# Selected-keys attention by groups of three heads, with fp32r logits and one wide values product

## The chip, the cores and the metric

The kernel runs on one core of a Trainium2 chip. The metric is the device time of one execution in microseconds (us). TensorE (PE) multiplies and transposes into PSUM, its weight loads are shown as PEld, VectorE is DVE, ScalarE is ACT, GpSimd is POOL, and SyncE (SP) issues the weight stream. TensorE's clock has two levels, 1.2 and 2.4 GHz; the profile gives it as a granted share, 0.50 or 1.00. fp32r is a float32 with fewer mantissa bits, which TensorE takes in one pass; a plain fp32 product takes four.

## What is computed

The reference is two transformer blocks over 1024 tokens of width 1024. The change touches one part of the first block, the selected-keys attention (six heads of 64 in two key groups, 128 queries at a time, 256 selected keys per query):

```
# one block of 128 queries
score = einsum('bqh,bqhs->bqs', wi_b, relu(einsum('bqhd,bsd->bqhs', qi_b, ki))) * idx_scale
score = where(causal, score, -inf)
_, sel = top_k(score, topk)                      # topk = 256
logits = einsum('bqgrd,bqkgd->bqgrk', qg, k_sel) * HEAD_DIM ** -0.5   # g: 2 groups, r: 3 heads
logits = where(valid, logits, -inf)
p = softmax(logits, axis=-1)
o = einsum('bqgrk,bqkgd->bqgrd', p, v_sel)
```

Everything else (projections, convolutions, memory attention, feed-forward, the second block) is computed by both kernels in the same way.

## The kernel before

All projections are weight-streaming products: SyncE loads a tile of weights, GpSimd splits it into two fp32r parts (`w_hi`, `w_lo`, lines 425 and 427), and TensorE multiplies them by the two parts of the activations (lines 516 to 520). Each engine has its own program, written out in order; they meet at semaphores, and in `meet` (line 383) all three wait for each other.

The attention is done densely. The scores of the index heads are reduced to a mask by 32 rounds of eight maxima (`topk_round`, line 1618), which VectorE runs beside the convolution tiles and the gate tiles. Then `L1694` turns the taken scores to 0 and the others to -1e30, the engines meet, and the stage that I call DSA begins: 48 steps, one for each block `i` of 128 queries and each head (`DSA_PLAN`), from 128 keys for block 0 to 1024 for block 7. A step n runs through the engines so:

- PE (lines 801 to 821): the logits of step n (`L809`, plain fp32, 64 rows, one or two banks of `side`), the transposes of the probabilities of step n-1 (`L736`, in `probs_turn`), the values product of step n-2 (`L819`, plain fp32, 128 columns for each key block).
- DVE (1697 to 1713): adds the mask and takes the row maximum into a strip `T` (`L1704`), negates it (`L1708`), waits for the exponential, inverts the sum (`L1710`), scales the strip (`L1712`).
- ACT (1192 to 1209): the exponential with its row sum (`L1196`), the copy of the transposed strips (`L1134`, in `copy_turned`), the head's output (`L1204`), and after six heads the rounding of the block (`L1208`); POOL takes the low part (`L486`).

Ahead of the stage ACT fetches the spilled gates (`fetch`) and the second memory input (`m_in`); behind it come the tiles of the attention's output projection. The convolution (`L1653` to `L1672` on DVE) and the gates (`gate_blocks`) stand before it.

## Time and profile before

| | us |
|---|---|
| median of 3 runs | 3167.75 (3165.0 to 3170.51) |
| the profiled execution | 3164.58 |
| its span | 3162.5 |
| PE busy | 2957.7 (94%) |
| DVE busy | 1713.8 (54%) |
| ACT busy | 768.3 (24%) |
| POOL busy | 1158.9 (37%) |
| mean granted clock of TensorE | 0.959 |

The views used further on are these. The page's chain follows the work that ended last back to the start. The stretches give the busy time of each engine between two times, with the granted clock. The timeline gives single instructions in order of time; "idle before" in brackets is how long the engine stood and who ended it. The groups by line give the mean duration of one instruction. A TensorE duration in a timeline contains the pipeline's tail, so what one matmul costs in a stream is the distance from start to start, or its share in the chain.

### The profile page before, as it was taken

The page shows a single profiled execution, that of the slowest core. Times are in us where ns is not written, and L with a number is a line of the kernel's source. Part 1 is how long each engine was busy: PE and PEld are TensorE (multiplying, and loading weights), DVE is VectorE, ACT ScalarE, POOL GpSimd, SP SyncE. Part 2 cuts the span into 40 slices and gives each one's busy share as a digit, 9 for nine tenths or more (in the row PEclk, how much of TensorE's full clock was granted, in tenths as well). Part 3 has the DMA queues.
Part 4 walks back from the last instruction along what each step waited for, and adds up shares of the span by engine and source line. Part 5 has one row for each costly group of instructions (what it writes and reads, how often), then busy time and mean ns, then how long its engine had stood idle before and what let it go on. Part 6 is the DMA issues. An engine that isn't in the chain of part 4 may idle for free.

```text
span 3162.5 us, 35461 instructions
## 1 busy us (share of the span) xinstructions
PE 2957.7 (94%) x13362; PEld 2385.8 (75%) x13362; DVE 1713.8 (54%) x2369; ACT 768.3 (24%) x1389; POOL 1158.9 (37%) x649
## 2 busy tenths in 40 slices
PE   7987999998989899999999879999888999999997
PEld 4675878885767688888888667887666888888885
DVE  4475899985552633242332647888948333333327
ACT  3054011113531311020110255666613000000002
POOL 2330434441023333344334415555532443334331
PEclk9978999996999999999999989999999999999998
DMA  3110112221031111111111210000020111111111
GB/s 144 41 34 7 47 67 80 80 80 67 1 133 67 34 47 54 47 46 46 53 46 47 67 74 27 21 27 27 21 80 27 54 47 47 52 46 46 47 53 60
DMA packets 45053, 165.40 MB, mean 52 GB/s; under 512 B 4880, under 2 KB 6160, under 8 KB 43920
## 3 DMA queue, kind: packets, MB, share of 16 engines
q1 hardware_dynamic: 37168, 129.31, 12.3%
q10 hardware_dynamic: 7776, 34.61, 2.8%
q8 instruction: 72, 1.18, 0.1%
q14 instruction: 37, 0.30, 0.0%
HBM read 147.12 MB, written 16.78 MB: 52 GB/s over the span
## 4 chain that ended last, share of the span: by engine, by line
PE 82%; DVE 11%; issue 3%; ACT 2%; DVEq 1%; POOL 0%; ACTq 0%; DMA 0%; SPq 0%; POOLq 0%
PE dense L516 21%; PE dense L520 20%; PE dense L517 20%; DVE stay L1914 2%; PE dense L904 2%; PE side L809 2%; PE dense L905 2%; PE dense L906 2%; PE dense L819 1%; DVE a_lo L1521 1%; PE dense L736 1%; PE dense L553 1%; PE side L942 1%; PE dense L554 1%; PE dense L555 1%
## 5 line engine op out<-in xcount | busy, mean ns | idle before, releaser
L425 POOL TENSOR_TENSOR w_hi<-raw,zero 128x1024 fp32r<-128x1024 f32 x210 | 401.1, 1910 | 1584.3 <-PE dense L520 1327.0
L516 PE MATMUL dense<-a_hi,w_hi 128*128 128x512 f32 x2000 | 786.0, 393 | 32.6 <-DVE T L1820 8.2
L517 PE MATMUL dense<-a_lo,w_hi 128*128 128x512 f32 x2000 | 781.9, 391 | 0.0
L520 PE MATMUL dense<-a_hi,w_lo 128*128 128x512 f32 x2000 | 618.9, 391 | 0.0
L427 POOL TENSOR_TENSOR w_lo<-raw,w_hi 128x1024 fp32r<-128x1024 f32 x210 | 524.9, 2499 | 16.5
L516 PEld LDWEIGHTS dense<-a_hi,w_hi 128*128 128x128 f32 x2000 | 378.2, 189 | 115.1 <-issue 14.9
L517 PEld LDWEIGHTS dense<-a_lo,w_hi 128*128 128x128 f32 x2000 | 378.1, 189 | 79.5 <-issue 1.2
L520 PEld LDWEIGHTS dense<-a_hi,w_lo 128*128 128x128 f32 x2000 | 377.5, 189 | 79.0
L516 PE MATMUL dense<-b_hi,w_hi 128*128 128x512 f32 x832 | 326.8, 393 | 4.0 <-DVE T L1820 2.5
L517 PE MATMUL dense<-b_lo,w_hi 128*128 128x512 f32 x832 | 324.4, 390 | 0.0
L1800 DVE TENSOR_TENSOR x_res<-x_res,dense 128x1024 f32<-128x1024 f32 x100 | 122.0, 1220 | 328.4 <-PE dense L520 327.0
L1820 DVE SCALAR_TENSOR_TENSOR T<-dense,tiny,T 128x1023 f32<-128x1023 f32 x88 | 112.8, 1282 | 295.1 <-ACT T L1259 291.6
L520 PE MATMUL dense<-b_hi,w_lo 128*128 128x512 f32 x832 | 256.7, 390 | 0.0
L475 POOL TENSOR_TENSOR stick_weights<-stick_weights,stay 128x511 f32<-128x511 f32 (+2 forms) x144 | 132.0, 917 | 174.8 <-DVE stay L1914 174.8
L516 PEld LDWEIGHTS dense<-b_hi,w_hi 128*128 128x128 f32 x832 | 156.4, 188 | 44.9 <-issue 4.8
L1411 ACT ACTIVATE b_hi<-T 128x1024 fp32r<-128x1024 f32 x32 | 34.0, 1062 | 610.1 <-DVE T L1995 610.1
L520 PEld LDWEIGHTS dense<-b_hi,w_lo 128*128 128x128 f32 x832 | 156.5, 188 | 32.8
L517 PEld LDWEIGHTS dense<-b_lo,w_hi 128*128 128x128 f32 x832 | 156.5, 188 | 31.7
L1259 ACT ACTIVATE T<-dense,tiny 128x1024 f32<-128x1024 f32 x44 | 49.2, 1117 | 518.5 <-PE dense L520 514.5
L1624 DVE MATCH_REPLACE8 score<-tiny,score 128x384 f32<-128x384 f32 (+2 forms) x192 | 165.7, 876 | 0.0
L1620 DVE MAX8 tiny<-score 128x8 f32<-128x384 f32 (+2 forms) x192 | 155.4, 877 | 3.1 <-issue 1.9
L1993 DVE TENSOR_SCALAR T<-dense 128x1024 f32<-128x1024 f32 x32 | 39.2, 1224 | 191.6 <-PE dense L520 190.6
(263 smaller groups left out, 4406.8 us busy)
## 6 DMA issues: line engine op xcount, KB each, us to landing
raw<-in_w_stream SPq DMA_DIRECT2D x231, 512.0 KB, 3.4
x_in<-in_x_t SPq DMA_DIRECT2D x8, 512.0 KB, 7.2
spill_gate<-T ACTq DMA_DIRECT2D x8, 512.0 KB, 2.6
spill_part<-gates ACTq DMA_DIRECT2D x8, 512.0 KB, 2.7
back<-spill_gate ACTq DMA_DIRECT2D x8, 512.0 KB, 3.8
back<-spill_part ACTq DMA_DIRECT2D x8, 512.0 KB, 4.8
x_res<-in_x_t ACTq DMA_DIRECT2D x2, 2048.0 KB, 9.5
spill_x<-x_res ACTq DMA_DIRECT2D x1, 4096.0 KB, 13.6
```

What stands on the lines that cost most here:

```text
L425: pool.tensor_tensor(w_hi[:, r % 2, :], raw[:, r, :], zero[:, 0:1].broadcast_to([P, D]), ALU.add).then_inc(weights_rounded, 1)
L427: pool.tensor_tensor(w_lo[:, r % 2, :], raw[:, r, :], w_hi[:, r % 2, :].bitcast(F32), ALU.subtract).then_inc(weights_split, 1)
L475: pool.tensor_tensor(w[:, 0:width - 1], w[:, 0:width - 1], stay[n % STRIPS][:, 1:width], ALU.mult).then_inc(w_ready, 1)
L516: pe.matmul(o, w_hi[:, slot, w], hi[:, k, x], start=b == 0, stop=False)
L517: pe.matmul(o, w_hi[:, slot, w], lo[:, k, x], start=False, stop=False)
L520: last = pe.matmul(o, w_lo[:, slot, w], hi[:, k, x], start=False, stop=stop)
L809: last = pe.matmul(side[:, n % 2, c:e], q_f[r, h % 3, i * P:i * P + P], k_f[r, c:e], start=True, stop=True)
L904: pe.matmul(o, w_hi[:, t % 2, w], a_hi[:, b, x], start=b == 0, stop=False)
L1620: dve.max(best[:, i - TOPK // P, :], score[:, score_at(i):score_at(i + 1)])
L1624: dve.match_replace(sc, best[:, i - TOPK // P, :], sc, TAKEN)
L1800: dve.tensor_tensor(x_res[:, n, :], x_res[:, n, :], dense[:, u % 2, :], ALU.add).then_inc(sums_free[u % 2], 1)
L1820: last = dve.scalar_tensor_tensor(T[:, slot, d:S], dense[:, u % 2, 0:S - d], tap, T[:, slot, d:S], ALU.mult, ALU.add)
```

## The change

DSA now goes by groups of three heads that share keys and values (16 groups: block `i`, key group `g`), and in a second kind of step, the turn: one key block of one group, 72 in all.

- Logits: the keys of a group are rounded to fp32r and stored above their own remainder (`k_stack`, 128 rows). The queries are rounded (`round_queries`, ACT) and their remainder is taken (`split_queries`, DVE), each written twice, for both halves of the rows. A head's logits are then two fp32r products over 128 rows instead of one fp32 product over 64 (`att_logits`).
- Turns: `att_turn` transposes one key block of three heads into one bank, one copy of 384 columns takes it to `pt` (every third on DVE, the others on ACT), and `att_values` multiplies it, plain fp32, with 384 columns, two turns later.
- Strips: nine of them, so maxima and exponentials run ahead of the turns. The first three groups are masked before the first turn; group s has its logits spread over the turns of group s-2 (`LOGITS_AT`), and its queries are rounded and split one turn before its first logits (`DUP_AT`).
- The mask (before: one instruction ahead of the barrier) is made in the stage, block by block. `m_in` is loaded after the stage. The keys and the first two groups of queries are split before the convolution and before the gates.

The diff, without tile allocations, semaphore names and two changed arguments:

```diff
@@ -92,8 +92,33 @@
 IDX_STEPS = (TB - TOPK // P) * IDX_H
-DSA_PLAN = [(i, h) for i in range(TB) for h in range(ATT_H)]
+DSA_PLAN = [(i, g) for i in range(TB) for g in range(GROUPS)]
 DSA_STEPS = len(DSA_PLAN)
+REP = ATT_H // GROUPS
+DSA_TURNS = [(s, kb) for s, (i, g) in enumerate(DSA_PLAN) for kb in range(i + 1)]
+DSA_X0 = [DSA_TURNS.index((s, 0)) for s in range(DSA_STEPS)] + [len(DSA_TURNS)]
+DSA_LEAD, DSA_LAG, DSA_STRIPS = 3, 2, 9
+def logits_at(s, j):
+    first, last = DSA_X0[s - 2] - 1, DSA_X0[s - 1] - 2
+    return first + (last - first) * j // (REP - 1)
+LOGITS_AT = {}
+for _n in range(REP * DSA_LEAD, REP * DSA_STEPS):
+    LOGITS_AT.setdefault(logits_at(_n // REP, _n % REP), []).append(_n)
+DUP_AT = {logits_at(s, 0) - 1: s for s in range(DSA_LEAD + 2, DSA_STEPS)}
+def on_dve(x):
+    return x % 3 == 2
+def copies_before(x):
+    return (x // 3, x - x // 3)[0 if on_dve(x) else 1]
 IDX_S = S - TOPK
...
@@ -798,27 +847,51 @@
-            for n in range(DSA_STEPS + 2):
-                if n < DSA_STEPS:
-                    i, h = DSA_PLAN[n]
-                    r = slice(HD * (h // 3), HD * (h // 3) + HD)
-                    if n >= 2:
-                        pe.wait_ge(lg_max, TB + n - 1)
-                    for c in range(0, P * (i + 1), 512):
-                        e = min(P * (i + 1), c + 512)
-                        last = pe.matmul(side[:, n % 2, c:e], q_f[r, h % 3, i * P:i * P + P], k_f[r, c:e], start=True,
-                                         stop=True)
-                    last.then_inc(lg_ready, 1)
-                if 1 <= n <= DSA_STEPS:
-                    probs_turn(n - 1, TB, DSA_PLAN[n - 1][0] + 1)
+            pe.wait_ge(k_low, GROUPS)
+            def att_logits(n):
+                s, j = n // REP, n % REP
+                i, g = DSA_PLAN[s]
+                pe.wait_ge(dup_split, s + 1)
                 if n >= 2:
-                    b = n - 2
-                    i = DSA_PLAN[b][0]
-                    pe.wait_ge(lg_tc, TB + b + 1)
-                    for kb in range(i + 1):
-                        last = pe.matmul(dense[:, b % 2, 0:P], v_f[:, kb, :], T[:, 2 + b % 2, kb * P:kb * P + P],
-                                         start=kb == 0, stop=kb == i)
-                    last.then_inc(lg_o, 1)
+                    pe.wait_ge(d_max, n - 1)
+                for c in range(0, P * (i + 1), 512):
+                    e = min(P * (i + 1), c + 512)
+                    pe.matmul(side[:, n % 2, c:e], qd_hi[:, s % 2, j, :], k_stack[:, g, c:e], start=True, stop=False)
+                    last = pe.matmul(side[:, n % 2, c:e], qd_lo[:, s % 2, j, :], k_stack[:, g, c:e], start=False, stop=True)
+                last.then_inc(d_ready, 1)
+            def att_turn(x):
+                s, kb = DSA_TURNS[x]
+                if kb == 0:
+                    pe.wait_ge(d_probs, REP * (s + 1))
+                if x >= 2:
+                    probs_copied(pe, x - 2)
+                for j in range(REP):
+                    last = pe.transpose(att_turn_bank(x)[:, j * P:j * P + P],
+                                        strips[(REP * s + j) % DSA_STRIPS][:, kb * P:kb * P + P], ident[:, :])
+                last.then_inc(d_turned, 1)
+            def att_values(x):
+                s, kb = DSA_TURNS[x]
+                if kb == 0 and s >= 2:
+                    pe.wait_ge(d_taken, s - 1)
+                probs_copied(pe, x)
+                pe.matmul(att_out_bank(s), v_f[:, kb, :], pt[:, x % 4, :], start=kb == 0, stop=kb == DSA_PLAN[s][0]
+                          ).then_inc(d_out, 1)
+            for n in range(REP * DSA_LEAD):
+                att_logits(n)
+            for x in range(len(DSA_TURNS) + DSA_LAG):
+                if x < len(DSA_TURNS):
+                    att_turn(x)
+                for n in LOGITS_AT.get(x, ()):
+                    att_logits(n)
+                if x >= DSA_LAG:
+                    att_values(x - DSA_LAG)
             meet(pe, "pe", met_n)
...
@@ -1140,6 +1213,17 @@
+            def round_queries(s):
+                i, g = DSA_PLAN[s]
+                if s >= 2:
+                    act.wait_ge(d_ready, REP * (s - 1))
+                for half in (g, 1 - g):
+                    last = act.activation(qd_hi[group_rows(half), s % 2, :, :], q_f[group_rows(g), :, i * P:i * P + P], ACT.Copy)
+                last.then_inc(dup_round, 1)
+            for g in range(GROUPS):
+                act.activation(k_stack[group_rows(g), g, :], k_f[group_rows(g), :], ACT.Copy).then_inc(k_round, 1)
             for j in range(3):
...
@@ -1148,6 +1232,9 @@
                 act.activation(yc_hi[:, j, :], T[:, 2, :], ACT.Copy).then_inc(parts["yc"][0], 1)
+            act.wait_ge(parts["yc"][1], 3)
+            for s in range(2):
+                round_queries(s)
...
@@ -1188,27 +1275,44 @@
             fetch(1)
-            act.dma_start(m_in[:, :, :], io["mem2_t"]).then_inc(mem2_loaded, 16)
-            for n in range(DSA_STEPS + 2):
-                if n < DSA_STEPS:
-                    w, e = P * (DSA_PLAN[n][0] + 1), n % 8
-                    act.wait_ge(lg_max, TB + n + 1)
-                    act.activation(T[:, n % 2, 0:w], T[:, n % 2, 0:w], ACT.Exp, bias=neg_max[:, e:e + 1], scale=SCALE,
-                                   accum_out=row_sum[:, e:e + 1]).then_inc(lg_exp, 1)
-                if 1 <= n <= DSA_STEPS:
-                    copy_turned(n - 1, TB, P * (DSA_PLAN[n - 1][0] + 1))
-                if n >= 2:
-                    i, h = DSA_PLAN[n - 2]
-                    r = slice(HD * (h // 3), HD * (h // 3) + HD)
-                    act.wait_ge(lg_o, TB + n - 1)
-                    act.activation(ya_f[r, h % 3, i * P:i * P + P], dense[r, n % 2, 0:P], ACT.Copy).then_inc(lg_oc, 1)
-                    if h == ATT_H - 1:
-                        act.wait_ge(lg_oc, TB + n - 1)
+            def exponentials(n):
+                w, e = P * (DSA_PLAN[n // REP][0] + 1), n % 8
+                act.wait_ge(d_max, n + 1)
+                act.activation(strips[n % DSA_STRIPS][:, 0:w], strips[n % DSA_STRIPS][:, 0:w], ACT.Exp, bias=neg_max[:, e:e + 1],
+                               scale=SCALE, accum_out=row_sum[:, e:e + 1]).then_inc(d_exp, 1)
+            for s in range(DSA_LEAD):
+                for j in range(REP):
+                    exponentials(REP * s + j)
+                    if j == 0:
+                        round_queries(s + 2)
+            for x in range(len(DSA_TURNS) + DSA_LAG + 1):
+                if x < len(DSA_TURNS) and not on_dve(x):
+                    act.wait_ge(d_turned, x + 1)
+                    if x >= 4:
+                        act.wait_ge(d_out, x - 3)
+                    act.activation(pt[:, x % 4, :], att_turn_bank(x), ACT.Copy).then_inc(d_copied_act, 1)
+                for n in LOGITS_AT.get(x, ()):
+                    exponentials(n)
+                if x in DUP_AT:
+                    round_queries(DUP_AT[x])
+                e = x - DSA_LAG - 1
+                if e >= 0 and e + 1 in DSA_X0:
+                    s = DSA_X0.index(e + 1) - 1
+                    i, g = DSA_PLAN[s]
+                    act.wait_ge(d_out, e + 1)
+                    act.activation(ya_f[group_rows(g), :, i * P:i * P + P],
+                                   att_out_bank(s)[group_rows(g), :].rearrange("p (j q) -> p j q", j=REP), ACT.Copy
+                                   ).then_inc(d_taken, 1)
+                    if g == GROUPS - 1:
+                        act.wait_ge(d_taken, s + 1)
                         act.activation(ya_hi[:, :, i * P:i * P + P], ya_f[:, :, i * P:i * P + P], ACT.Copy
+            act.dma_start(m_in[:, :, :], io["mem2_t"]).then_inc(mem2_loaded, 16)
...
@@ -1650,6 +1754,19 @@
+            def split_queries(s):
+                i, g = DSA_PLAN[s]
+                dve.wait_ge(dup_round, s + 1)
+                for half in (g, 1 - g):
+                    last = dve.tensor_tensor(qd_lo[group_rows(half), s % 2, :, :], q_f[group_rows(g), :, i * P:i * P + P],
+                                             qd_hi[group_rows(g), s % 2, :, :].bitcast(F32), ALU.subtract)
+                last.then_inc(dup_split, 1)
+            for g in range(GROUPS):
+                dve.wait_ge(k_round, g + 1)
+                dve.tensor_tensor(k_stack[group_rows(1 - g), g, :], k_f[group_rows(g), :],
+                                  k_stack[group_rows(g), g, :].bitcast(F32), ALU.subtract).then_inc(k_low, 1)
             for j in range(3):
...
@@ -1670,6 +1787,8 @@
                 low((yc_hi[:, j, :], yc_lo[:, j, :]), j, T[:, 2, :], "yc", j + 1)
+            for s in range(2):
+                split_queries(s)
...
@@ -1690,27 +1809,53 @@
-            sc = score[:, score_at(2):score_at(TB)]
-            dve.tensor_scalar(sc, sc, TAKEN / 2, NEG, ALU.is_gt, ALU.mult)
             meet(dve, "dve", met_n)
-            for n in range(DSA_STEPS):
-                i, e = DSA_PLAN[n][0], n % 8
+            def mask(n):
+                s, e = n // REP, n % 8
+                i = DSA_PLAN[s][0]
                 w = P * (i + 1)
-                dve.wait_ge(lg_ready, TB + n + 1)
-                if n >= 2:
-                    dve.wait_ge(lg_t, TB + n - 1)
-                dve.tensor_tensor_reduce(out=T[:, n % 2, 0:w], in0=side[:, n % 2, 0:w],
-                                         in1=score[:, score_at(i):score_at(i) + w], scale=1.0, scalar=TAKEN, op0=ALU.add,
-                                         op1=ALU.max, accum_out=row_max[:, e:e + 1])
+                sc = score[:, score_at(i):score_at(i) + w]
+                if i >= TOPK // P and n % (REP * GROUPS) == 0:
+                    dve.tensor_scalar(sc, sc, TAKEN / 2, NEG, ALU.is_gt, ALU.mult)
+                    dve.drain()
+                dve.wait_ge(d_ready, n + 1)
+                if s >= 3:
+                    dve.wait_ge(d_turned, DSA_X0[s - 2])
+                dve.tensor_tensor_reduce(out=strips[n % DSA_STRIPS][:, 0:w], in0=side[:, n % 2, 0:w], in1=sc, scale=1.0,
+                                         scalar=TAKEN, op0=ALU.add, op1=ALU.max, accum_out=row_max[:, e:e + 1])
                 dve.drain()
-                dve.tensor_scalar(neg_max[:, e:e + 1], row_max[:, e:e + 1], -SCALE, None, ALU.mult).then_inc(lg_max, 1)
-                dve.wait_ge(lg_exp, TB + n + 1)
+                dve.tensor_scalar(neg_max[:, e:e + 1], row_max[:, e:e + 1], -SCALE, None, ALU.mult).then_inc(d_max, 1)
+            def normalise(n):
+                w, e = P * (DSA_PLAN[n // REP][0] + 1), n % 8
+                dve.wait_ge(d_exp, n + 1)
                 dve.reciprocal(inv_sum[:, e:e + 1], row_sum[:, e:e + 1])
                 dve.drain()
-                dve.tensor_scalar(T[:, n % 2, 0:w], T[:, n % 2, 0:w], inv_sum[:, e:e + 1], None, ALU.mult
-                                  ).then_inc(lg_p, 1)
+                dve.tensor_scalar(strips[n % DSA_STRIPS][:, 0:w], strips[n % DSA_STRIPS][:, 0:w], inv_sum[:, e:e + 1], None,
+                                  ALU.mult).then_inc(d_probs, 1)
+            for n in range(REP * DSA_LEAD + 2):
+                if n < REP * DSA_LEAD:
+                    mask(n)
+                    if n % REP == 0:
+                        split_queries(n // REP + 2)
+                if n >= 2:
+                    normalise(n - 2)
+            for x in range(len(DSA_TURNS)):
+                if on_dve(x):
+                    dve.wait_ge(d_turned, x + 1)
+                    if x >= 4:
+                        dve.wait_ge(d_out, x - 3)
+                    dve.tensor_copy(pt[:, x % 4, :], att_turn_bank(x)).then_inc(d_copied_dve, 1)
+                for n in LOGITS_AT.get(x, ()):
+                    mask(n)
+                for n in LOGITS_AT.get(x - 1, ()):
+                    normalise(n)
+                if x in DUP_AT:
+                    split_queries(DUP_AT[x])
             meet(dve, "dve", met_n)
```

The order of TensorE before, in block 7: logits of a head, transposes of the one before, values of the one before that. `side` holds logits, `T` probabilities, `v_f` values.

```order
L809 MATMUL side<-k_f,q_f 128x512 [waits row_max_ready]
L809 MATMUL side<-k_f,q_f 128x512
L736 MATMUL dense<-ident,T 128x128 [waits heads_copied,probs_ready]
L736 MATMUL dense<-ident,T 128x128 x7
L819 MATMUL dense<-T,v_f 128x128 [waits probs_copied]
L819 MATMUL dense<-T,v_f 128x128 x6
```

The order of TensorE now, from the last head of the fourteenth group (896 keys) to the first of the fifteenth (1024 keys): `strip` holds probabilities, `att_probs_t` the copied turns, `qd_hi` and `qd_lo` the queries.

```order
L861 MATMUL side<-k_stack,qd_hi 128x512 [waits att_row_max_ready,queries_split]
L862 MATMUL side<-k_stack,qd_lo 128x512
L861 MATMUL side<-k_stack,qd_hi 128x384
L862 MATMUL side<-k_stack,qd_lo 128x384
L883 MATMUL dense<-att_probs_t,v_f 128x384 [waits att_probs_copied_dve]
L873 MATMUL dense<-ident,strip_108 128x128 [waits att_probs_copied_act]
L873 MATMUL dense<-ident,strip_109 128x128
L873 MATMUL dense<-ident,strip_110 128x128
L861 MATMUL side<-k_stack,qd_hi 128x512 [waits att_row_max_ready,queries_split]
L862 MATMUL side<-k_stack,qd_lo 128x512
```

One turn of values and transposes stands between the last logits of a group and the next group's, which wait for `queries_split`.

The order of VectorE before, one head of 896 keys and the start of the next (`ISA` is the masking with its maximum):

```order
L1704 ISA T,tiny<-side,score 128x896 [waits probs_turned,logits_ready]
L1704 ISA tiny 128x1
L1708 TENSOR_SCALAR tiny<-tiny 128x1
L1710 RECIPROCAL tiny<-tiny 128x1 [waits exp_ready]
L1712 TENSOR_SCALAR T<-T,tiny 128x896
L1704 ISA T,tiny<-side,score 128x896 [waits probs_turned,logits_ready]
```

The order of VectorE now, at the same two heads as TensorE's rows, from the last head of 896 keys to the first of 1024:

```order
L1826 ISA strip_107,tiny<-side,score 128x896 [waits att_probs_turned,att_logits_ready]
L1826 ISA tiny 128x1
L1829 TENSOR_SCALAR tiny<-tiny 128x1
L1762 TENSOR_TENSOR qd_lo<-q_f,qd_hi 64x384 [waits queries_rounded]
L1762 TENSOR_TENSOR qd_lo<-q_f,qd_hi 64x384
L1852 COPY att_probs_t<-dense 128x384 [waits att_values_done,att_probs_turned]
L1821 TENSOR_SCALAR score<-score 128x1024
L1826 ISA strip_108,tiny<-side,score 128x1024 [waits att_probs_turned,att_logits_ready]
L1826 ISA tiny 128x1
L1829 TENSOR_SCALAR tiny<-tiny 128x1
L1835 RECIPROCAL tiny<-tiny 128x1 [waits att_exp_ready]
L1837 TENSOR_SCALAR strip_107<-strip_107,tiny 128x896
```

The split of the next group's queries stands between the maximum of the last head and its normalisation, and waits for `queries_rounded`; on ScalarE the rounding stands behind that head's exponential.

## Rows read from the trace of the kernel before

**Rows 1.** The page, part 4: shares of the chain that ended last, by engine.

```profile
PE 82%; DVE 11%; issue 3%; ACT 2%; DVEq 1%; POOL 0%; ACTq 0%; DMA 0%; SPq 0%; POOLq 0%
```

**Rows 2.** Stretches: us, busy us and instructions by engine, PE clock, DMA.

```profile
735.10:796.80 61.70, 57.15 (x167) 36.45 (x168) 24.12 (x105) 27.33 (x85) 2.98 (x3) 0.50 0.15 55
796.80:904.80 108.00, 103.92 (x626) 75.69 (x626) 52.49 (x135) 58.81 (x117) 4.99 (x5) 1.00 0.00 1
```

**Rows 3.** Chain, at the lower and full clock: start us, us, what.

```profile
767.82 0.85 PE dense L819 x4
...
858.06 0.92 PE dense L736 x7
858.97 1.56 PE dense L819 x14
860.54 1.70 PE side L809 x4
```

**Rows 4.** Timeline of a head: start us, us, engine, line, what, idle.

```profile
849.96 1.09 DVE L1704 CUSTOM_DVE_ANT_0 T<-side,score 128x896 f32<-128x896 f32 x1 [0.38 <-PE side L809]
851.32 1.04 ACT L1196 ACTIVATE T<-T,tiny 128x896 f32<-128x896 f32 x1 [1.57 <-DVE tiny L1708]
852.48 0.16 DVE L1710 RECIPROCAL tiny<-tiny 128x1 f32<-128x1 f32 x1 [1.20 <-ACT T L1196]
852.73 0.69 DVE L1712 TENSOR_SCALAR T<-T,tiny 128x896 f32<-128x896 f32 x1
```

**Rows 5.** By line, 600 to 1200 us: busy us, mean ns, idle.

```profile
L1704 DVE CUSTOM_DVE_ANT_0 T<-side,score 128x1024 f32<-128x1024 f32 x6 | 7.3, 1224 | 5.2 <-PE side L809 5.2
L1704 DVE CUSTOM_DVE_ANT_0 T<-side,score 128x128 f32<-128x128 f32 x6 | 1.7, 288 | 1.5 <-PE side L809 1.5
L1196 ACT ACTIVATE T<-T,tiny 128x1024 f32<-128x1024 f32 x6 | 6.9, 1149 | 12.7 <-DVE tiny L1708 12.7
L1196 ACT ACTIVATE T<-T,tiny 128x128 f32<-128x128 f32 x6 | 2.4, 401 | 4.6 <-DVE tiny L1708 4.6
L1712 DVE TENSOR_SCALAR T<-T,tiny 128x1024 f32<-128x1024 f32 x6 | 4.5, 753 | 0.8 <-issue 0.4
L1712 DVE TENSOR_SCALAR T<-T,tiny 128x128 f32<-128x128 f32 x6 | 1.7, 287 | 0.5
L1208 ACT ACTIVATE ya_hi<-ya_f 128x384 fp32r<-128x384 f32 x8 | 4.2, 524 | 0.2
L1830 DVE TENSOR_TENSOR b_lo<-T,b_hi 128x1024 fp32r<-128x1024 f32 x4 | 4.9, 1225 | 4.5 <-ACT b_hi L1264 4.5
```

**Rows 6.** A stretch of the gates, PE in fp32r only.

```profile
480.00:560.00 80.00, 80.00 (x355) 66.26 (x354) 78.50 (x131) 7.94 (x12) 34.43 (x16) 1.00 0.24 83
```

**Rows 7.** Timeline where the stage begins.

```profile
730.54 4.49 DVE L1694 TENSOR_SCALAR score<-score 128x4224 f32<-128x4224 f32 x1
730.65 0.34 ACTq L1175 DMA_DIRECT2D spill_part<-gates  x1
737.85 1.28 ACT L1196 ACT_TABLE_LOAD   x1 [15.93 <-issue]
```

**Rows 8.** Stretches in and behind two gaps of PE.

```profile
403.70:407.80 4.10, 0.00 (x0) 0.00 (x0) 4.06 (x9) 0.00 (x0) 3.85 (x2) 0.98 0.00 0
409.30:414.70 5.40, 5.36 (x13) 4.24 (x14) 4.54 (x4) 0.43 (x1) 0.00 (x0) 0.52 0.27 97
902.70:904.80 2.10, 0.02 (x1) 0.00 (x0) 0.00 (x0) 0.79 (x2) 0.99 (x1) 1.00 0.00 0
906.00:909.20 3.20, 3.20 (x10) 2.44 (x9) 0.00 (x0) 0.00 (x0) 0.00 (x0) 0.50 0.00 0
```

**Rows 9.** The page, part 6: issues, KB each, us to landing.

```profile
spill_part<-gates ACTq DMA_DIRECT2D x8, 512.0 KB, 2.7
```

**Rows 10.** VectorE's waits in the two stages ahead.

```profile
327.65 1.22 DVE L1659 TENSOR_TENSOR T<-dense,T 128x1024 f32<-128x1024 f32 x1 [3.92 <-PE dense L520]
...
448.90 1.22 DVE L1685 TENSOR_TENSOR gates<-dense,gates 128x1024 f32<-128x1024 f32 x1 [1.67 <-PE dense L520]
```

25 lines of the change are left out of this document (22 added, 3 removed).

## The prediction, made before the result was known

> **What bounds the kernel now.** I read first the page's chain: TensorE (PE) carries 82% of what ended last [rows 1]. A change elsewhere counts only where PE waits for it. Then the stretches [rows 2]: the stage of the change (DSA, the selected-keys attention) runs from 735.1 to 904.8 us, 169.7 us, with VectorE busy 76.6 us and ScalarE 86.1 us. Up to 796.8 PE's granted clock is 0.50 (1.2 GHz), after it 1.00 (2.4 GHz). In the chain of that stage [rows 3] a head of 896 keys is 0.92 us of transposes, 1.56 of values, 1.70 of logits, end to end: 4.18 us, all PE. At the low level two blocks of values take 0.85, twice as long each. So PE bounds each head here: the four-pass fp32 products do, not the waits. Last the timeline of one head [rows 4]: row maximum at 849.96, exponential from 851.32, reciprocal at 852.48, probabilities ready at 853.42. VectorE sits 1.20 us behind the exponential in each head. Before the change that is hidden, since PE has the last head's values and the next head's logits to do.
>
> **What each piece costs.** Linear in width between the rows for 128 and 1024 keys [rows 5]:
> - M, logits ready to maximum ready: 0.29 to 1.22 for the reduction, 0.23 for accumulator and negation (849.96 to 851.32, less 1.09 and a hop of 0.04 [rows 4]): 0.52 to 1.46.
> - E, maximum ready to VectorE's reciprocal: the exponential plus 0.16 (851.32 to 852.48 for one of 1.04, and the hop): 0.56 to 1.31.
> - N, the normalisation: 0.25 to its start [rows 4] and 0.29 to 0.75: 0.54 to 1.00.
> - R, round_queries: two ScalarE copies of 64x384. The nearest row, 128x384, has 0.52: 1.0. Bounds: 0.8 (two at the 0.40 of a 128-wide exponential) to 1.2.
> - S, split_queries: two VectorE subtractions of 64x384. 1024 columns take 1.23; less 640 at the reduction's 1.04 ns each leaves 0.56: 1.12. Bounds: 0.6 (the 128-wide reduction's 0.29 a piece) to 2.5 (1.23 a piece).
> - A copy of turned strips, 128x384 out of PSUM: 0.5 on ScalarE, by the same row of 0.52; on VectorE 0.55, where the reduction, also a read of PSUM, has 384 columns.
> - L, logits of one head in fp32r: PE does 355 matmuls of 512 in 80 us at the full clock [rows 6], 0.225 each, so four are 0.90 for 1024 keys, where fp32 took 1.70 for 896. About 0.2 for 128 keys.
> - A turn (one key block, three heads): transposes 3 x 0.13 = 0.39, values 3 x 0.22 less the saved loads = 0.65: 1.04. The bounds of the 384-column product are 0.34 (two records at an fp32r matmul's 0.44 ns a column) and 0.67; I take 0.65, because the fp32 block of 128 is the same arithmetic.
>
> Sums: PE has 72 turns x 1.04 = 75 and 27648 columns of logits in two passes, 25: 100 us at the full clock. VectorE has 48 heads at (M + N + 0.05), 83; 24 copies, 13; 14 splits, 16; the score mask, 5: 117. ScalarE is near 98. By totals alone the stage would be 120 to 140 us. That is not what the order of the instructions gives.
>
> **The new wait.** The queries of a group are rounded and split right behind the last head of the group before, and the logits of the new group wait for that (queries_split). The rows of the order show it. The chain for each group from the sixth to the last, eleven times, is: L, then 0.2 until VectorE starts, M, E, R, S, 0.1 for two hops, and only then the next logits. For 1024 keys: 0.9 + 0.2 + 1.46 + 1.31 + 1.0 + 1.12 + 0.1 = 6.1 us; for 512: 4.7. Behind its last logits PE has one values product and one turn's transposes (1.04 us), and then its next matmul is the waiting one: it idles 6.1 - 0.9 - 1.04 = 4.1 us at 1024, about 3.2 at 512. Queued behind it are all turns, values and copies of the stage. The rounding is queued behind the exponential, the split behind the rounding, so nothing overlaps. In the chain of before no piece passes another: transposes, values and logits of three different heads follow in the order written [rows 3].
> The Trainium skill ("TensorE: Matmul & The Clock Gate", Part 2, step 1) says that only weight loads are pulled ahead while matmuls stay in program order. By that rule the turns behind the wait can't fill the gap and the sum stands; if PE could pass it, 11 gaps of some 3.7 us, 40 us, would go. The trace agrees with the rule.
>
> A second, smaller coupling: ScalarE's copy of turn x+1 stands behind the exponential of turn x, and the transposes of turn x+3 need it. From the logits of one head to those of the next, three turns later, at 1024: 0.9 + 0.2 + 1.46 + 1.31 + 0.5 (copy) + 0.4 (transposes) = 4.8 us, where PE alone has 0.9 + 3 x 1.04 = 4.0.
>
> **The sum, at the full clock.** Time from a group's first logits to the next group's:
> - 384 keys: two M of 0.79, one N of 0.67, a copy's share (2.6) and the chain of 4.4: 7.0
> - 512: two (M + N) of 0.92 + 0.74, 3.4 with hops, the chain 4.7, copy and mask 0.6: 8.7
> - 640: two M and three N, 4.7, the chain 5.2, copy and mask 0.8: 10.7
> - 768: two heads that VectorE walks through one by one (M + E + N = 3.2 each), 6.4 + 5.5 + 0.4 = 12.3
> - 896: to the third head's logits 1.0, then one M + E + N of 3.5 and one wait for ScalarE's copy of 3.5, 8.1; the chain 5.8: 13.9
> - 1024: two of the 4.8 above and the chain of 6.1: 15.7
>
> Before, three heads took 3 x 4.18 = 12.5 us at 896. The groups of 384 keys once, 512 to 896 twice each and 1024 once make 7.0 + 2 x (8.7 + 10.7 + 12.3 + 13.9) + 15.7 = 114. Ahead stands the lead-in, VectorE's: 15 maxima (six of 128, six of 256, three of 384 keys, 10.5 with the hops), 14 normalisations (8), four splits (4.5), one copy and twice a wait for logits (2), and its waits for ScalarE: 3.2 at the first split, because the DMA issues and the table load of 1.28 [rows 7] stand before the first exponential, and 5 for later roundings: 33 us. At the end the last group's heads (9.6), then its last logits, 17 turns, one wait for a copy and the last two values (0.9 + 17.7 + 1 + 1.3 = 21), and the same 2.1 us from PE's end to the next stage as before [rows 8]. Total 33 + 114 + 9.6 + 21 + 2.1 = 180 us, 10 more than before, though PE's own work is down to 100 us.
>
> **The clock.** The rows [rows 8] show what such gaps do: idle 403.7 to 409.3, then 0.50 until about 414.7; idle 902.7 to 904.8, then 0.50 from 906.0 to 909.2. So after a gap of 3 to 4 us I expect some 4.4 us at 1.2 GHz (the rows have 3.2 and 5.4), in which PE does half: 2.2 lost, a little of it covered by ScalarE's copies, 1.9 net. Nine groups: 17. The two smallest groups fit into the slow stretch whole, 3 more. Total 20, so the stage is 200 us.
>
> **The edits around it.** The score mask, 4.49 us of VectorE alone before the barrier [rows 7], moves into the stage. Instead the barrier waits for the spill issued at 730.65, 2.7 us to landing [rows 9]: it opens near 733.4, not 735.1, a gain of 1.7. Splitting the keys (two 64x1024, 2.5 us and the wait for ScalarE) ends before VectorE's wait of 3.92 us for PE; the first two query splits (3.3) fall on its wait of 1.67 before the first gate product and on the one behind it [rows 10]. PE waits for neither: zero, at most 2. Loading mem2 after the stage costs ScalarE an issue while it waits: zero; at most 1 if it delays the fetches.
>
> Profiled execution before: 3164.58. Stage +30.3, barrier -1.7: 3193.2. The median shown is 3.2 above that execution: **3196**.
>
> A second rule: "VectorE: DVE Perf Modes", section "Why PSUM operands drop a tier", in the Trainium skill, gives a copy out of PSUM the single rate, where one inside SBUF may go double. My row agrees: the normalisation in SBUF grows by 0.52 ns a column, the reduction from PSUM by 1.04. At the SBUF rate the 24 copies would be 3 us less, which moves no case.
>
> **Rivals.**
> 1. The clock holds at 2.4 GHz through the gaps. For: from 796.8 to 904.8 it held, with PE busy 103.9 of 108 us, so short waits leave it alone [rows 2]. Against: gaps of 2 and 4 us did not [rows 8]. Stage 180, 3176.
> 2. The clock stays at 1.2 GHz throughout, as from 735 to 797, where PE was busy 57 of 61.7 us and it did not rise [rows 2]. Periods are then PE's doubled work plus the gap: 8.1, 11.0, 14.3, 17.0, 20.0, 23.1; with tail: 247. 3243.
> 3. Faster: the split chain doesn't bind, because rounding and splitting cost near their lower bounds and exponentials hide behind turns; then the engines' totals bind (VectorE 117 plus the end on PE, 140). 3136. It decides if the chain takes under about 2 us more than the turns it stands beside. For: the totals. Against: every link is a measured duration in a fixed order.
> 4. The change does nothing that counts: chain and saved logits cancel, within 6 us of before. It needs the chain 1 us shorter in each group and no clock loss.
>
> **Chances.** Mine 0.46 (alone 3180 to 3215), rival 1 0.18, rival 2 0.11, rival 3 0.19, rival 4 0.06. Faster or slower means by over 0.2%, 6 us, about what a measurement tells: faster 0.19, same 0.06, slower 0.75. The range must hold rival 1, most of 2 and the bounds of R and S (11 x 1 us down, 11 x 1.6 up): 3150 to 3242.
>
> **What would show it.** Right: in the stage's waits PE idles behind the query split (about eleven times, 3 to 4 us, at its logits), VectorE behind ScalarE's rounding; the stage lasts near 200 us with PE under 75% busy, its clock switching in each group; logits of 512 at 0.23 us apart. Wrong: a stage under 165 us, VectorE over 80% busy in it, or no PE wait over 2 us.

## The result, and the profile after

The changed kernel takes 3191.62 us (median of 4 runs, 3189.02 to 3193.12), the kernel before 3168.66 (4 runs): ratio 1.0070, 95% interval 1.0058 to 1.0083, 18 to 26 us slower. The predicted time was 3196, and slower had 0.75. The profiled execution took 3191.37 us, span 3189.5.

The page's chain [rows 1] reads, after the change:

```profile
PE 81%; DVE 11%; issue 3%; ACT 3%; DVEq 1%; POOL 0%; DMA 0%; ACTq 0%; SPq 0%; POOLq 0%
```

All shares are within a point of those before, so that line hides what happened. The stretches of the stage [rows 2] show it (us, busy us and instructions of PE, PEld, DVE, ACT, POOL, granted clock, DMA share, GB/s):

```profile
735.00:758.00 23.00, 9.77 (x32) 7.65 (x33) 12.75 (x61) 10.91 (x31) 0.00 (x0) 0.50 0.32 114
758.00:798.00 40.00, 27.04 (x102) 19.19 (x102) 28.24 (x91) 21.90 (x54) 2.01 (x2) 0.80 0.00 1
798.00:890.00 92.00, 62.81 (x250) 43.26 (x249) 52.52 (x126) 42.52 (x86) 4.00 (x4) 0.85 0.00 1
890.00:920.10 30.10, 26.15 (x127) 16.77 (x125) 10.54 (x23) 13.53 (x27) 1.99 (x2) 1.00 0.02 3
735.00:920.10 185.10, 125.76 (x505) 86.87 (x505) 104.05 (x298) 88.86 (x197) 8.01 (x8) 0.82 0.04 15
```

The stage takes 185.1 us instead of 169.7, although PE is busy 35 us less than before (125.8 against 161.1). PE's waits in it (engine, tile, line, released by: us in total, times, longest):

```profile
PE side L861 <- DVE qd_lo L1762: 40.3, 11, 4.5
PE side L861 <- DVE tiny L1829: 13.1, 8, 4.4
PE side L861 <- ACTq L435: 5.9, 1, 5.9
PE dense L873 <- ACT att_probs_t L1296: 3.4, 3, 1.8
```

The first row is the new wait of the prediction, eleven times. One of its chains from the trace, for 896 keys, to be read beside the head of before [rows 4] (start us, us, engine, line, what, idle before and its releaser):

```profile
862.98 0.48 PE L861 MATMUL side<-k_stack,qd_hi 128*128 128x512 f32 x1
...
864.09 1.09 DVE L1826 CUSTOM_DVE_ANT_0 strip<-side,score 128x896 f32<-128x896 f32 x1 [0.28 <-PE side L862]
...
864.53 0.49 PE L873 MATMUL dense<-ident,strip 128*128 128x128 f32 x3
...
865.45 1.04 ACT L1283 ACTIVATE strip<-strip,tiny 128x896 f32<-128x896 f32 x1 [1.49 <-DVE tiny L1829]
...
866.49 1.04 ACT L1222 ACTIVATE qd_hi<-q_f 64x384 fp32r<-64x384 f32 x2
867.57 1.12 DVE L1762 TENSOR_TENSOR qd_lo<-q_f,qd_hi 64x384 fp32r<-64x384 f32 x2 [2.15 <-ACT qd_hi L1222]
...
868.74 0.50 PE L861 MATMUL side<-k_stack,qd_hi 128*128 128x512 f32 x1 [3.72 <-DVE qd_lo L1762]
```

Logits, maximum, exponential, rounding, split, logits: 5.76 us from 862.98 to 868.74, where the prediction's pieces give 5.8. PE's last work in it is three transposes at 864.53, then nothing for 3.72 us. For 1024 keys the chain is 6.25 (880.18 to 886.43, predicted 6.1) and the idle time 4.10 (predicted 4.1).

The stage explains 15.4 us, not all 27.0 that lie between the two spans. Ahead of it nothing is left over: 735.2 and 735.0. Behind it the kernel before and the changed one read:

```profile
904.86:3162.50 2257.64, 2134.77 (x9684) 1743.41 (x9684) 1084.88 (x1286) 526.68 (x915) 896.66 (x522) 0.97 0.15 51
```
```profile
920.10:3189.50 2269.40, 2143.99 (x9684) 1748.42 (x9684) 1086.42 (x1286) 527.65 (x915) 896.97 (x522) 0.97 0.15 51
```

The counts are the same on every engine, the code is the same, and it takes 11.8 us longer. PE is busy 9.2 us longer with the same 9684 matmuls, so most of it is slower matmuls; the other 2.6 us are waits, in small pieces. The same gap of PE in both, in the feed-forward, and what follows it (stretch, its length, PE busy and matmuls, granted clock, DMA share, GB/s), before and after:

```profile
1072.10:1080.30 8.20, 0.00 (x1) 0.78 0.39 128
1080.30:1082.80 2.50, 2.46 (x6) 0.50 0.00 0
1082.80:1085.30 2.50, 2.50 (x11) 0.86 0.00 0
```
```profile
1091.55:1099.75 8.20, 0.00 (x1) 0.69 0.41 130
1099.75:1102.25 2.50, 2.46 (x6) 0.50 0.00 0
1102.25:1104.75 2.50, 2.50 (x8) 0.50 0.00 0
```

The gap is 8.2 us in both. Behind it the clock comes back after some 3 us in the one and not within 5 us in the other: 17 matmuls in 5 us against 14. Reading the granted clock in slices of 2.5 us over the whole part, it was at 0.50 for 113 us in all before and for 135.5 us after. PE works at half its speed in that time, so half of the difference, 11.3 us, is about the time that is missing. The prediction had no such term.

### The profile page after: what moved, and what is told of

The parts are those of the page before. It is cut to its first block, busy times and chain, and to the rows that moved or that the text cites. A ratio compares the mean times of both kernels' runs of the same rounds, so it can differ in the third digit from the quotient of the medians.

```text
span 3189.5 us, 35000 instructions
## 1 busy us (share of the span) xinstructions
PE 2932.1 (92%) x13074; PEld 2366.9 (74%) x13074; DVE 1740.1 (55%) x2432; ACT 776.6 (24%) x1391; POOL 1158.4 (36%) x649
## 3 DMA queue, kind: packets, MB, share of 16 engines
q1 hardware_dynamic: 37168, 129.31, 12.1%
q8 instruction: 70, 1.15, 0.1%
## 4 chain that ended last, share of the span: by engine, by line
PE 81%; DVE 11%; issue 3%; ACT 3%; DVEq 1%; POOL 0%; DMA 0%; ACTq 0%; SPq 0%; POOLq 0%
PE dense L565 21%; PE dense L566 20%; PE dense L569 20%; DVE stay L2059 2%; PE dense L977 2%; PE dense L978 2%; PE dense L979 2%; PE dense L602 1%; DVE a_lo L1625 1%; PE dense L603 1%; PE dense L604 1%; PE side L1015 1%; PE dense L883 1%; ACT T L1187 1%; PE side L635 1%
```

## The experiments

Numbers of the stage run from PE's first logits to the first product of the output projection, as above. "Low" is the time that the granted clock was at 0.50, from slices of 2.5 us.

**Is the chain the cause? The duplication one group earlier** (with this, PE's program is unchanged; ScalarE and VectorE round and split behind the first head of the group before).

```
-DUP_AT = {logits_at(s, 0) - 1: s for s in range(DSA_LEAD + 2, DSA_STEPS)}
+DUP_AT = {logits_at(s - 1, 0): s for s in range(DSA_LEAD + 2, DSA_STEPS)}
```

> The rounding and the split of a group's queries are issued behind the first head of the group before, not behind its last one; nothing else is moved. Theory 1 (the serial chain from a group's last logits to the next group's first is what PE waits for, 11 times, 40 us in the trace of the changed kernel): the waits of PE behind qd_lo (L1762) nearly go, below 5 us in sum. What comes next is VectorE, which now stands behind the exponential and the rounding inside the group before (2.3 us a time, of which about half is in PE's shadow), so some 25 of the 40 us come back: stage 160 us, kernel near 3166. Rival (the wait only shows where VectorE, ScalarE and PE together would be late anyway): the idle time moves to the transposes and the logits behind row maxima, and the stage stays within 5 us of 185: 3187 or more.

Measured: 3164.25 us, ratio to before 0.9982 (0.9973 to 0.9992), stage 162.5, low 32 us of it (66 in the changed kernel). PE's waits in the stage:

```profile
PE dense L873 <- ACT att_probs_t L1296: 20.1, 19, 2.7
PE side L861 <- DVE tiny L1829: 15.5, 11, 4.3
PE dense L873 <- DVE att_probs_t L1852: 6.7, 5, 2.0
...
PE side L861 <- DVE qd_lo L1762: 1.6, 1, 1.6
```

One line of the plan takes 22.6 us out of the stage and turns a loss of 0.7% into a gain of 0.2%. The wait for the split falls from 40.3 to 1.6 us; the rival is out. What came next is not VectorE, as I expected, but the prediction's second coupling: transposes that wait for a copy which ScalarE issues behind an exponential.

**Ahead of the exponential and the maximum too.**

```
                 for n in LOGITS_AT.get(x, ()):
-                    exponentials(n)
-                if x in DUP_AT:
-                    round_queries(DUP_AT[x])
+                if x in DUP_AT:  round_queries(DUP_AT[x])      # and on VectorE split_queries before mask
+                for n in ...:    exponentials(n)
```

> As the run with the early rounding and split, but within their step they also stand ahead of the exponential and of the row maximum, so that they wait for no new logits. Theory 1: VectorE waits for the rounding only (1.0 us), in a stretch in which PE has turns to do: stage 150 us, kernel near 3156. Rival (the engines' coupling sets the pace, whatever the place of the split): within 5 us of the changed kernel, 3187.

Measured: 3174.80 us, ratio 1.0008 (0.9998 to 1.0018), stage 171.5, low 60. I expected a stage of 150: a miss. PE's largest waits:

```profile
PE dense L873 <- ACT att_probs_t L1296: 23.2, 12, 4.3
PE side L861 <- DVE tiny L1829: 19.9, 12, 4.5
```

VectorE's waits for the rounding are still 18.9 us in all (from 760 us on), and they now stand ahead of the maxima. The move only changed what waits: rounding and split (1.04 + 1.12) now stand between the logits and their maximum, the exponential comes that much later, and the copy behind it too. Waits of up to 4.3 us at the transposes let the clock fall, as the chain's had.

**One half alone: grouped turns, plain fp32 logits.**

```
-pe.matmul(side[:, n % 2, c:e], qd_hi[:, s % 2, j, :], k_stack[:, g, c:e], start=True, stop=False)
-last = pe.matmul(side[:, n % 2, c:e], qd_lo[:, s % 2, j, :], k_stack[:, g, c:e], start=False, stop=True)
+last = pe.matmul(side[:, n % 2, c:e], q_f[group_rows(g), j, i * P:i * P + P], k_f[group_rows(g), c:e],
+                 start=True, stop=True)      # and no rounding, no split, no wait for them
```

> One half of the change alone: groups of three heads, 384-column values product and copies by two engines, but the logits stay a plain fp32 product of the 64-row queries and keys; keys and queries are neither rounded nor split. Theory 1: no chain, PE has 75 us of turns and 27648 columns at 1.9 ns, 52 us, 127 at the full clock; with a lead-in of some 25 us that runs partly beside it and at the low level the stage takes 150 to 155 us, kernel near 3158, below the kernel before (3168). Rival: the grouped turns themselves cost (copies of 384 columns on a path that is blocked by exponentials), then the stage stays at 175 or more, 3180.

Measured: 3179.41 us, ratio 1.0024 (1.0014 to 1.0035), stage 175.7. The theory (150 to 155) missed it. The rival's numbers came (175 or more, 3180), but not for its reason, since PE waits little for copies. Its stage in two stretches, and that wait:

```profile
733.55:803.50 69.95, 68.23 (x136) 32.13 (x137) 34.00 (x141) 27.23 (x72) 2.27 (x2) 0.53 0.11 38
803.50:909.20 105.70, 100.12 (x369) 54.05 (x368) 54.47 (x129) 47.34 (x98) 5.98 (x6) 0.95 0.01 1
```
```profile
PE dense L871 <- ACT att_probs_t L1288: 3.2, 4, 1.6
```

There is no chain here and PE is busy 168.4 of 175.7 us. Its work at the full clock is about 130 (168.4 less half of the 77 us at the low level; 127 expected), the same as in the kernel before (161.1 less half of 61.6): the wide product alone saves PE nothing. The clock stays at 0.50 for 66 us of nearly unbroken work, as it did in the kernel before [rows 2], and falls once more for 10 us at 868. With the split logits it rises at 760, PE being far less busy. Beside this run the one with the early duplication, which differs in the logits and their preparation alone, has a stage 13 us shorter: half of what the fp32r logits save PE by the prices worked out ahead (25 us where fp32 takes 52), since there PE waits more (busy 114.2 of 162.6 us).

**What does the clock cost in the stage? Gaps filled with products.**

```
+FILL = dict(zip(range(5, DSA_STEPS), (15, 7, 10, 9, 14, 11, 16, 13, 13, 12, 14)))
 if n >= 2:
     pe.wait_ge(d_max, n - 1)
+for _ in range(FILL.get(s, 0) if j == 0 else 0):
+    pe.matmul(side[:, n % 2, 0:512], qd_hi[:, (s - 1) % 2, j, :], k_stack[:, g, 0:512], start=True, stop=True)
 pe.wait_ge(dup_split, s + 1)          # moved behind the wait for the maximum
```

> In front of the eleven waits for the split queries PE does 7 to 16 products of 512 columns whose result is overwritten (134 in all, 30 us at 0.225, each gap filled to within some 0.8 us). The waits stay, the clock has no reason to fall. The prediction gave the clock 20 us of the stage; the trace of the changed kernel, whose stage of 185.1 us is 5 above the 180 worked out for the full clock, says about 5. Theory 1 (the chain is paced by VectorE and ScalarE, the low clock falls mostly on work in their shadow): granted clock near 1.00 from 770 us on, stage 178 to 182, kernel 3184 to 3189. Rival (the low clock costs what the prediction said): stage near 168, kernel 3172. Third: the products themselves overrun the gaps, stage 187 or more.

Measured: 3172.22 us, ratio 1.0006 (0.9996 to 1.0016), 19 us faster than the changed kernel with 134 matmuls more. That total is the rival's 3172, but only 12.4 us of it come from the stage; 4.4 lie behind it and 2.3 ahead of it. The whole stage, and the stretch in which the gaps lie:

```profile
732.70:905.45 172.75, 140.62 (x639) 99.11 (x639) 102.51 (x298) 87.81 (x197) 8.04 (x8) 0.93 0.05 16
757.70:880.00 122.30, 106.86 (x496) 75.58 (x496) 81.18 (x216) 63.87 (x139) 6.04 (x6) 1.00 0.00 1
```

From 758 us on the clock holds at 1.00 and the stage is 12.4 us shorter. The chain itself does not change: at 1024 keys it is 6.24 us here (866.41 to 872.65), 6.25 without the products. So the low clock cost 12.4 us in the stage, between my 5 and the prediction's 20, and the prediction's stage at the full clock, 180, was too long by 7. (The first 25 us of this stage are still at the low clock, as in the changed kernel.)

**Is the chain serial? Each split done twice** (the first into a tile nobody reads, from the sixth group on).

```
 dve.wait_ge(dup_round, s + 1)
+for half in (g, 1 - g) if s >= 5 else ():
+    dve.tensor_tensor(T[group_rows(half), half, 0:REP * P].rearrange("p (j q) -> p j q", j=REP),
+                      q_f[group_rows(g), :, i * P:i * P + P], qd_hi[group_rows(g), s % 2, :, :].bitcast(F32), ALU.subtract)
```

> The changed kernel with each split from the sixth group on done twice (the first time into a tile nobody reads): 11 times two more subtractions of 0.552 us, all directly behind the rounding. Theory (rounding, split and logits are one serial chain that sets the pace): at least 11 x 1.1 = 12.1 us on the stage of 185.1, and on the time (3191.6 to 3204 or a little above, for longer gaps at the low clock). Rival (the chain is only partly on the path): 6 us or less.

Measured: stage 202.1, 16.3 above the 185.8 of the changed kernel's second profile; 12.1 was put in. The wait:

```profile
PE side L861 <- DVE qd_lo L1766: 54.3, 11, 5.9
```

From 40.0 in that second profile to 54.3, all of what was put in and the clock's share on top (low 87 us instead of 70). The time rose less, from 3190.20 to 3199.25: behind the stage this kernel took 2261.0 us and the changed one 2269.1, with the same instructions. The total shows 9 us where the stage has 16.

**The second coupling: exponentials one turn later.** On top of the early duplication (the rounding, too, moves ahead of the exponentials of its turn):

```
-for n in LOGITS_AT.get(x, ()):          exponentials(n)     # ScalarE
 if x in DUP_AT:      round_queries(DUP_AT[x])
+for n in LOGITS_AT.get(x - 1, ()):      exponentials(n)
-for n in LOGITS_AT.get(x - 1, ()):      normalise(n)        # VectorE
+for n in LOGITS_AT.get(x - 2, ()):      normalise(n)
-if x in DUP_AT:      split_queries(DUP_AT[x])
+if x - 1 in DUP_AT:  split_queries(DUP_AT[x - 1])
```

> As the run with rounding and split behind the first head of the group before, and beside that ScalarE issues each exponential one turn later, VectorE each normalisation and each split one turn later, so that the copy of a turn no longer stands behind an exponential that waits for fresh logits. In that run PE waited 20.1 us at its transposes for ScalarE's copies. Theory (this second coupling is what is left on the path, as the prediction's 4.8 us against 4.0 a head at 1024 keys had it): those waits fall under 6 us, stage 147 to 152 us where it was 162.5, kernel near 3152. Rival (VectorE is the bound by then, or the waits move to the row maxima): stage within 4 us of 162.5, kernel 3161 or more.

Measured: 3140.83 us, ratio 0.9906 (0.9890 to 0.9923), stage 140.2. The wait for ScalarE's copies is gone:

```profile
PE dense L873 <- ACT att_probs_t L1296: 0.9, 2, 0.5
```

22 us for an order in which nothing is computed differently; I expected 10 to 15. The run moves exponentials, normalisations, rounding and split together, and doesn't say how much each is worth; the waits for ScalarE's copies were 20.1 us of what there was to gain.

**Fetches behind the first exponentials.** `fetch(0)` and `fetch(1)` move from ahead of `exponentials(0)` to behind those of the second and third group.

> As the run with the late exponentials, and ScalarE issues its four fetches of spilled tiles behind the exponentials of the second and third group, not ahead of the first. In the changed kernel they take ScalarE from 735.05 to 736.96 us while everything waits for the first exponential. Theory (the lead-in up to the sixth group is the serial walk of VectorE and ScalarE): 1.9 us less, stage and kernel. Rival: the lead-in is paced otherwise, the issues come back as waits later, no change within 1 us.

Measured: 3138.95 us, ratio 0.9903 (0.9887 to 0.9920), stage 139.9 against 140.2: the rival holds. The first exponential comes only 0.4 us earlier (738.33 against 738.72), because ScalarE's table load now waits for the first maximum:

```profile
737.03 1.28 ACT L1280 ACT_TABLE_LOAD   x1 [13.02 <-DVE tiny L1828]
```

**The lead-in.** On top of that:

```
+act.activation(bias_now[:, :], bias_now[:, :], ACT.Exp)     # behind the gates, ahead of the waits for the spills
-                    if n % REP == 0:
+                    if n % REP == 1:
                         split_queries(n // REP + 2)
```

> As the run with the fetches behind, and two moves in the lead-in: ScalarE's table for the exponential is loaded by a small exponential before the barrier, while the last spill is landing (1.28 us), and VectorE does the splits of the third to fifth group behind the second row maximum of a group, not behind the first, so that the second maximum no longer waits for exponential and rounding (VectorE waited 3.3 us at the first of these splits). Theory (the lead-in is VectorE's and ScalarE's serial walk): 3 to 4 us less in the stage, 136, kernel near 3135. Rival (the low clock and other waits fill it again): within 1 us.

Measured: 3138.91 us, ratio 0.9904 (0.9879 to 0.9928). The stage is the shortest of all:

```profile
733.57:870.04 136.47, 109.86 (x504) 76.25 (x505) 103.11 (x298) 86.65 (x196) 8.14 (x8) 0.91 0.06 20
```

3.5 us less than in the run before, as expected; the 3135 expected for the kernel did not come, since the part behind the stage took 2267.3 us instead of 2260.9. These last three are some 30 us or 1% faster than the kernel before and some 50 faster than the changed one; which of them is best the totals can't tell.

**The part behind the stage.** Three runs: the kernel before and the changed one once more, and the kernel before made longer (`for c in list(range(0, P * (i + 1), 512)) * 9` at the last head, which computes its logits nine times).

> The kernel before, unchanged, for a second profile of it. Theory (luck of the execution): its part behind the stage differs from the 2257.6 us of the first profile by several us, at the same instructions, and by half of the difference in low-clock time. Rival (each kernel has its own fixed pattern): 2257.6 within 1 us, and low for 113 us.

> The changed kernel, unchanged, for a second profile and more executions of it. The two profiles of the kernel before agree in the stage (169.7 and 169.6) and differ by 1.4 us behind it. Theory (the stage is 15 us longer, and how long the clock stays low behind it adds a few us that vary): stage 182 to 188, behind it 2262 to 2270, the time of most executions within 3187 to 3194. Rival (the 185.1 was a fluke of one execution): stage below 180 or above 190.

> The kernel before with nothing changed but 16 more fp32 products of 512 columns in front of its last head's logits (the same logits computed nine times; at 1.7 us for 896 keys about 0.97 each, 15.5 us). It moves everything behind the stage by as much as the change did. In the profiles the part behind the stage took 2257.6 us before and 2269.4 in the changed kernel, with the same instructions; the granted clock was low for 112.8 and 135.5 us in it. Theory (how long the clock stays low behind each gap varies from one execution to the next, and the profiled execution of before was a lucky one): the median rises by 15.5 us, 3186, no more. Rival (the shift itself lengthens the low stretches): it rises by 20 to 27 us, 3191 to 3197.

| kernel | time, median | stage | behind it | of that at the low clock |
|---|---|---|---|---|
| before, first profile | 3168.66 | 169.7 | 2257.6 | 113 |
| before, second profile | 3168.25 | 169.6 | 2259.0 | 114 |
| changed, first profile | 3191.62 | 185.1 | 2269.4 | 135.5 |
| changed, second profile | 3190.20 | 185.8 | 2269.1 | 132 |
| before, made longer | 3185.81 | 183.4 | 2266.6 | 135.5 |
| gaps filled | 3172.22 | 172.7 | 2265.0 | 125 |
| early duplication | 3164.25 | 162.5 | 2262.3 | 116 |
| ahead of the exponential | 3174.80 | 171.5 | 2269.6 | 135.5 |
| plain logits | 3179.41 | 175.7 | 2268.2 | 135 |
| split twice | 3199.25 | 202.1 | 2261.0 | 120 |
| exponentials later | 3140.83 | 140.2 | 2264.7 | 119 |
| fetches later | 3138.95 | 139.9 | 2260.9 | 109 |
| lead-in | 3138.91 | 136.5 | 2267.3 | 129 |

All of these do the same work behind the stage, with the same 9684 matmuls. It takes between 2257.6 and 2269.6 us. Between the two kernels half of the difference in low-clock time is nearly all of it. Over all rows it is not: less half of their low time the parts still lie between 2199 (made longer) and 2206 (fetches later), and with the fetches later there is less low time than in the kernel before, yet the part takes 3.3 us more. Nor does the part grow with the length of the stage. The stages of both kernels repeat to 0.7 us. The part behind it repeated too, to 1.4 and 0.3 us: that is nearer to the rival of the second profile of before (within 1 us) than to my theory of luck (several us), though neither range was met. But both profiled executions of before (3164.58 and 3165.45) lie 3 to 6 us below the medians (3168 to 3171) of some 60 runs, which spread from 3159.4 to 3174.7, so two profiles say little of its middle. The longer kernel got a stage 13.8 us longer, not 15.5, and a median 16.8 us above that of before (ratio 1.0048, 1.0032 to 1.0065): 3 us more than the stage, inside the interval. That median is what the theory gave (3186), and the rival's 3191 did not come; but its profile, against that of before, has 8.9 us more behind the stage, as the rival had it. Whether the shift itself lengthens the low stretches stays open.

## Why the prediction was nearly right

The direction and the mechanism were right; the size, 3196 against 3191.6, came out of errors that cancel. The prediction had 30.3 us for the stage and a gain of 1.7 ahead of it; the spans of the two profiles show 15.4 for the stage, 0.2 gained ahead of it and 11.8 behind it, where the prediction had nothing. That 28.6 and 27.0 agree is luck. By its steps:

1. **PE bounds the stage before, and the products saved are not what counts.** Right. PE's busy time fell by 35 us and the stage grew.
2. **The chain.** Right in every link: split 0.552 a piece (0.56 taken), rounding 1.04 the pair (1.0), exponential 1.15 and reduction 1.23 at 1024, the copy 0.56 and 0.48 to 0.49 (0.55 and 0.5), 5.76 and 6.25 us in sum (5.8 and 6.1). Eleven waits of 2.4 to 4.5 us, 40.3 in sum (40 by the prediction's 11 gaps of 3.7); logits of 512 columns follow at 0.23 us, and PE is busy 68% of the stage. That the chain is the cause is shown: moved away, the stage loses 22.6 us; made longer by 12.1, it gains 16.3.
3. **The sum at the full clock, 180 us.** 172.7 with the gaps filled. From first logits of a group to those of the next, by the prediction, in the changed kernel and with filled gaps:

| keys | predicted | changed | filled | exponentials later |
|---|---|---|---|---|
| 384 | 7.0 | 7.9 | 6.5 | 6.2 |
| 512 | 8.7, 8.7 | 9.4, 9.2 | 8.4, 8.1 | 6.0, 6.7 |
| 640 | 10.7, 10.7 | 10.3, 12.1 | 10.3, 10.0 | 7.1, 8.4 |
| 768 | 12.3, 12.3 | 13.4, 12.8 | 12.2, 12.0 | 7.6, 9.0 |
| 896 | 13.9, 13.9 | 14.1, 14.0 | 12.8, 12.5 | 10.9, 9.1 |
| 1024 | 15.7 | 17.7 | 16.9 | 10.3 |
| sum | 113.9 | 120.8 | 109.5 | 81.4 |

   The periods were 4 us too long in sum, the lead-in 2.6 (33 against 30.4); the end was right (32.7 against 32.8). Most of it is at 896 keys (1.1 and 1.4 too long) and at 512 and 640 (2 in all), and 1024 was 1.2 too short; at 768, where I let VectorE walk the heads one by one, the sum fits. Why 896 came out shorter was not looked into. A turn too was dearer on paper: 1.04 against 0.97 (898.09 to 899.06, below). In the totals, VectorE's 48 heads at the prediction's own prices are 87 us and not 83; only rival 3 rests on them. The last column shows what the chain, the coupling and their low clock cost together: 39 us.

```profile
898.09 0.81 PE L883 MATMUL dense<-att_probs_t,v_f 128*128 128x384 f32 x2
898.73 0.49 PE L873 MATMUL dense<-ident,strip 128*128 128x128 f32 x3
899.06 0.81 PE L883 MATMUL dense<-att_probs_t,v_f 128*128 128x384 f32 x2
```

4. **The clock, 20 us.** The step that failed in size: 12.4. The clock fell in or just behind ten of the eleven waits, 41 us in all, so rival 1 and rival 2 are out. It did not fall at the wait of 3.00 us that ends at 792.15. The first of these stretches, and the one around 792.15:

```profile
763.60:770.40 6.80, 4.79 (x13) 3.68 (x14) 3.69 (x13) 3.33 (x9) 0.00 (x0) 0.50 0.00 1
788.00:798.00 10.00, 7.00 (x37) 4.91 (x36) 7.52 (x22) 4.91 (x12) 0.00 (x0) 1.00 0.00 0
```

   So the time at the low clock was sized well (4.1 us a stretch, 4.4 taken); its cost was not. 1.9 net for each gap was taken as if PE set the pace behind it. The runs show 1.1 a gap: 11.3 us over ten periods, 0.9 in the tail and 0.2 in the lead-in. PE is busy 37.6 of the 41 us, so half speed alone would have cost 18.8. The likely reason for the rest is that VectorE and ScalarE set part of the pace between the gaps and so cover a slow PE; that is argued from the chain and not tested by itself. The Trainium skill ("TensorE: Matmul & The Clock Gate", section "HAM oscillation — how this bites in real kernels") counts the cost of the low clock as half of the time spent at it. By that rule, as an estimate, the 41 us of low clock that the filled gaps took away (66 to 25) were worth 20; the runs show 12.4. Behind the stage, where PE is busy 94% of the time, the rule fits these two kernels: half of 22.7 is 11.3, and 11.8 are missing.
5. **The edits around.** The barrier opened when the spill had landed, 2.8 us behind its issue at 732.18, and the mask is inside the stage: 1.8 us gained between the last gate's end and the stage, as predicted (1.7). It is not in the total, because the part ahead came 1.5 us later, with 2 to 3 us more at the low clock; in the second profile the stage starts at 733.6.
6. **What the prediction left out.** 11.8 us behind the stage between the two profiles, in code that the change doesn't touch. By medians (3191.6 and 3190.2 against 3168.3 to 3170.6) the kernel is 20 to 23 us slower, so that beyond the stage's 15.5 some 4 to 8 us are to be explained, and the two profiles overstate them, since both of before lie below its median.

Rival 3, faster because the chain doesn't bind, is refuted for this kernel. What it predicted from the engines' totals comes true once the order is changed: 136.5 us, within the 120 to 140 that the prediction gave for totals alone.

Open stays why the clock comes back sooner or later behind the same gap, and why it does so alike in two profiles of one kernel.

## What to carry to other kernels

When work moves to other engines, follow one group through all of them in program order: a preparation issued behind the last consumer of the previous group puts every engine in one serial line, and totals say nothing. Prepare one group ahead, but behind what the critical engine waits for, and let no copy that frees a buffer stand behind an operation that waits for fresh results. Judge an edit of half a per cent by the stretch it touches, in two profiles, and not by the total alone.

## What the runs showed of the hardware

The low clock behind one and the same gap of 8.2 us lasted some 3 us in one kernel and over 5 in another; over the 2260 us behind the stage that makes up to 12 us. Products whose result nobody reads, done while PE waits anyway, gave 12.4 us in a stage of 185. And PE stayed at 1.2 GHz for 66 us of nearly unbroken work (busy 64.7) in the stage's first part with 64-row fp32 logits, while with 128-row fp32r logits the clock rose at 760, 25 us into a stage whose first 23 us had PE busy 9.8. The rows show the level that was granted, not what set it.
